# A hybrid decoder layer on eight cores: channel-major residual, measured durations in the order's planner, late weights in new places

## What is computed

```
x = x + 0.5 * swiglu(rmsnorm(x, ffn1_norm), w1, w3, w2)        # D_FF 2816
h = rmsnorm(x, mix_norm)
u = h @ w_in                                                   # q k v gate lru_x lru_gate
y_ret = (silu(g_ret) * head_groupnorm(retention(rotary(q), rotary(k), v))) @ w_ret_o
y_lru = (rg_lru(causal_conv(x_lru)) * gelu(g_lru)) @ w_lru_o
gates = sigmoid(h @ w_branch_gate + b)
x = x + (gates[:D] * y_ret + gates[D:] * y_lru) @ w_out
p = softmax((rmsnorm(x, xattn_norm) @ w_xq) (m @ w_xk)^T / 16) # m = rmsnorm(mem), 256 tokens, 4 heads
x = x + (p (m @ w_xv)) @ w_xo
x = x + 0.5 * swiglu(rmsnorm(x, ffn2_norm), ...)
out = rmsnorm(x, final_norm)
```

## Time and profile before

| | us |
|---|---|
| three runs, median (lowest to highest) | 1814.12 (1813.47 to 1816.82) |
| span of the profiled execution, slowest core | 1809.7 |
| spans of the eight cores | 1798.3 to 1809.7 |
| PE busy | 1713.9 (95%) |
| DVE, ACT, POOL busy | 879.6, 660.4, 374.8 |

### The profile page before, as it was taken

How to read it: one execution, slowest core, us unless ns; L and a number is a source line. 1 busy time by engine, 2 the same in 40 slices (tenths; PEclk the granted TensorE clock), 3 DMA queues, 4 the chain that set the end, 5 groups by cost and what they waited for, 6 DMA issues and landing times.

```text
span 1809.7 us, 24417 instructions; the slowest of 8 cores (1798.3 to 1809.7 us)
## 1 busy us (share of the span) xinstructions
PE 1713.9 (95%) x8432; PEld 815.1 (45%) x8600; DVE 879.6 (49%) x1309; ACT 660.4 (36%) x1016; POOL 374.8 (21%) x423
## 2 busy tenths in 40 slices
...
GB/s 223 133 60 75 105 153 83 28 78 122 146 257 16 85 54 58 49 43 49 36 24 47 110 197 78 83 191 48 12 71 12 49 45 1 70 36 12 7 93 93
DMA packets 56263, 141.62 MB, mean 78 GB/s; under 512 B 5968, under 2 KB 18256, under 8 KB 54096
## 3 DMA queue, kind: packets, MB, share of 16 engines
...
HBM read 168.87 MB, written 33.55 MB: 112 GB/s over the span
## 4 chain that ended last, share of the span: by engine, by line
PE 89%; DMA 3%; DVE 3%; issue 2%; ACT 1%; POOL 0%; SPq 0%; DVEq 0%; ACTq 0%; POOLq 0%
PE bank L636 86%; PE bank L847 1%; DMA X<-x 1%; DMA TW_107<-w_tail 1%; DMA X<-park 1%; DVE HB L839 0%; DMA XW<-w_xqT 0%; PE bank L1299 0%; DVE XC L1132 0%; DVE SC L1262 0%; PE bank L1302 0%; DVE T_88 L1210 0%; DVE T_88 L1208 0%; DVE SG L1315 0%; PE bank L1331 0%
## 5 line engine op out<-in xcount | busy, mean ns | idle before, releaser
L636 PE MATMUL bank<-hT,W_45 128*128 128x512 bf16 x2755 | 613.4, 379 | 4.3 <-DVE hT L855 1.0
L636 PEld LDWEIGHTS bank<-hT,W_45 128*128 128x128 bf16 x2816 | 275.2, 98 | 328.9 <-issue 2.8
L652 ACT ACTIVATE STMP<-bank 128x512 f32<-128x512 f32 x176 | 104.9, 596 | 597.0 <-PE bank L636 573.9
L636 PE MATMUL bank<-W_46,HID 128*128 128x512 bf16 x1378 | 311.1, 380 | 2.7 <-DVE HID L918 1.0
L936 DVE SCALAR_TENSOR_TENSOR X<-bank,X 128x512 f32<-128x512 f32 x256 | 175.3, 689 | 190.9 <-PE bank L636 174.2
L918 DVE TENSOR_TENSOR HID<-bank,STMP 128x512 bf16<-128x512 f32 x176 | 120.1, 690 | 299.7 <-PE bank L636 288.8
L636 PEld LDWEIGHTS bank<-W_46,HID 128*128 128x128 bf16 x1408 | 137.3, 98 | 164.3 <-issue 3.1
L652 ACT ACTIVATE JUNK<-X 128x1024 bf16<-128x1024 f32 x80 | 84.4, 1055 | 130.6 <-DVE X L936 63.7
L831 POOL TENSOR_TENSOR stat<-stat,cst 128x1 f32<-128x1 f32 x82 | 48.0, 587 | 351.7 <-DVE stat L830 349.7
L636 PE MATMUL bank<-hT,LW 128*128 128x512 bf16 x500 | 114.9, 382 | 0.6
L665 POOL DMA_DIRECT2D W_45<-f_w x44 | 23.9, 547 | 404.0 <-PE bank L636 393.9
...
## 6 DMA issues: line engine op xcount, KB each, us to landing
W_45<-f_w POOLq DMA_DIRECT2D x44, 512.0 KB, 7.1
...
X<-x SPq DMA_DIRECT2D x16, 512.0 KB, 10.6
park<-X SPq DMA_DIRECT2D x16, 512.0 KB, 9.0
X<-park SPq DMA_DIRECT2D x16, 512.0 KB, 23.1
out<-OST SPq DMA_DIRECT2D x16, 512.0 KB, 2.6
...
```

The source lines that it names most:

```text
L636: ins = e.matmul(out_ap, l, r, start=(start and i == 0), stop=(stop and i == n - 1), skip_group_check=skip)
L652: P.add("act", lambda e: e.activation(out, in_, func, **kw), reads=reads, writes=writes, cost=act_cost(n, nap), tab=tab)
```

## The change

- **X is channel-major**: `x`, `mem`, `out` and `park` come in a layout of [block, 128 channels, 8, 512 tokens]. `norm` works on a block of 512 tokens (256 for the first two blocks of FFN 1, for `mem`, and for the last block of the final norm): Squares to bf16 on ACT, sums over the 8 channel groups on DVE, one matmul with ones for the sum over partitions, Ln and Exp on ACT into `RSN`, eight products with a gain column on DVE (L995) straight into `hT`. No transposes, no gain rows, no POOL step. `w2`, `w_out` and the attention output have the weights stationary and the tokens moving.
- **Cross-attention**: scores with tokens on partitions, a maximum per head (DVE), Exp with an accumulated sum per head and 128 tokens (ACT, 256 wide), reciprocal and four products on DVE, eight transposes on PE, an eviction on ACT (`PX`); four buffers of `PEX` instead of two.
- **First loads**: the first two blocks of x come as four quarters of 256 tokens, alternating with the weights of FFN 1; the first hidden blocks are computed on halves of 256 tokens in the order of the expected arrivals. The last `w2` of FFN 2 is split into two halves of tokens. A one-element Exp loads ACT's table before the first norm, another after the last Silu.
- **Places**: `RW0` and `RW1` change sides (96 KB and 0), `TW` lies at 120, 0, 4, 64 and 68 KB, `GIN` and `WO` move too; the loads of `WO` wait for a `TW`.
- **Planner**: hand-overs are counted by pairs of engines (480 ns from PE to ACT, 530 to DVE, and 200 more for anything that PE waits for), operations on one engine overlap a little, DVE and POOL exclude each other in some operations, `TAB_HOLD` is 0, a bank class may be dealt out up to 6 ahead, and 24 passes are made, each with keys from a pass backward over the last plan; the shortest is kept.
- `NRAW` is 0 and `FPOOL` is empty, so the code for `raw`, `keep`, `later` and `pool_chunks` adds nothing.

```diff
 SEM_NS = 70.0
-DMA_NS_PER_B = 1.0 / 215.0
+LAT = {("pe", "act"): 480.0, ("pe", "dve"): 530.0, ("pe", "pool"): 900.0, ("pe", "sp"): 450.0, ("pe", "pe"): 0.0}
+LAT_TO = {"pe": 115.0, "act": 95.0, "dve": 103.0, "pool": 145.0, "sp": 80.0}
+OVL = {"pe": 0.0, "act": 46.0, "dve": 79.0, "pool": 31.0, "sp": 0.0}
+MARGIN = {"pe": 200.0}
+DMA_NS_PER_B = 1.0 / 285.0
 DMA_LAT = 2500.0
 TAB_NS = 1283.0
-TAB_HOLD = 600.0
+TAB_HOLD = 0.0
+LOOK = 6
+PASSES = 24
...
     def schedule(self):
+        best = None
+        keys = None
+        for it in range(PASSES):
+            plan = self.one_pass(keys)
+            if best is None or self.span < best[0]:
+                best = (self.span, plan, self.order)
+            keys = self.backward(plan)
+        self.span, plan, self.order = best
+        return plan
...
+    def lat_of(self, d, s):
+        k = LAT.get((d.eng, s.eng))
+        if k is None:
+            k = LAT_TO[s.eng]
+        if d.eng == "dve" and s.eng == "dve" or d.eng == "act" and s.eng == "act" or d.eng == "pool" and s.eng == "pool":
+            k = 20.0
+        if s.eng == "pe" and d.eng != "pe":
+            k += MARGIN["pe"]
+        return k
...
-            if c.q[c.i] != v or not free or c.use >= c.cap:
+            if not free or len(c.held) >= c.cap:
                 return None
+            if c.q[0] != v:
+                if v not in c.q[:c.look]:
+                    return None
+                if len(c.held) + max(0, c.keep - sum(1 for x in c.held if x < c.q[0])) >= c.cap:
+                    return None
...
-    def rstd_of(src_ap, src_hs, j):
...
-        jk = JUNK.v()
-        act(jk.ap, src_ap, AF.Square, src_hs, jk.hs + hs, D, accum=s[:, 0:1])
-        dve(lambda e: e.tensor_scalar(s[:, 1:2], s[:, 0:1], 1.0 / D, EPS, ALU.mult, ALU.add), hs, hs, 1)
-        pool(lambda e: e.tensor_tensor(s[:, 2:3], s[:, 1:2], cc(2), ALU.pow), hs + cst.hs, hs, 550)
...
+        for q in range(0 if ones else 4):
+            x = src(2 * q, 2)
+            d = part(2 * q, 2)
+            act(d.ap, x.ap, AF.Square, x.hs, d.hs, 2 * n)
+            if q:
+                dve(lambda e, d=d: e.tensor_tensor(acc.ap, acc.ap, d.ap, ALU.add), acc.hs + d.hs, acc.hs, 2 * n, 0.55)
...
+        r = keep if keep is not None else RSN.v((i % 2) * TB, n)
+        act(r.ap, banks[b][:, 0:n], AF.Ln, [hbk[b]] + cst.hs, r.hs, n, tab=S_LN, bias=cc(0), scale=1.0 / D)
+        act(r.ap, r.ap, AF.Exp, r.hs, r.hs, n, tab=S_EXP, scale=-0.5)
...
+                x = src(c, 1)
+                d = dst(c)
...
+                else:
+                    dve(lambda e, x=x, d=d, g=gc(c): e.scalar_tensor_tensor(d.ap, x.ap, g, r.ap, ALU.mult, ALU.mult),
+                        x.hs + r.hs + gcol.hs + list(after), d.hs, n, 1.148)
...
-                        pairs.append((hd.ap[:, j * 128:(j + 1) * 128], w.ap[:, half * 512:(half + 1) * 512]))
+                        pairs.append((w.ap[:, oc * 128:(oc + 1) * 128], hd.ap))
...
                     pend = [a for a in pend if a[1] % 2 not in [tb % 2 for tb in tbs]]
+                    first = halves and g == 0 and tbs[0] == 0
+                    if first:
+                        units = []
+                        for m, t in itertools.product(range(G), range(2)):
+                            if m < FULL[t]:
+                                units += [(m, t, 256 * hf, 256, 2 * t + hf) for hf in range(2)]
+                            else:
+                                units.append((m, t, 0, TB, 2 * t + 1))
+                        units.sort(key=lambda u: (max(ARR_W[u[0]], ARR_X[u[4]]), u))
...
-    GIN = [A.buf("GIN%d" % i, o * KB, F16, 2 * T) for i, o in enumerate((112, 64, 72, 80))]
-    TW = [A.buf("TW%d" % i, o * KB, BF16, 2 * KC * 128) for i, o in enumerate((120, 88, 92, 112, 116))]
-    WO = A.buf("WO", 96 * KB, BF16, KC * D)
+    GIN = [A.buf("GIN%d" % i, o * KB, F16, 2 * T) for i, o in enumerate((16, 8, 72, 80))]
+    TW = [A.buf("TW%d" % i, o * KB, BF16, 2 * KC * 128) for i, o in enumerate((120, 0, 4, 64, 68))]
+    WO = [A.buf("WO%d" % i, o * KB, BF16, D) for i, o in enumerate((88, 90, 92, 94, 164, 166, 198, 200))]
...
-            if oc == 2:
-                for k in range(KC):
-                    v = WO.v(k * D, D)
-                    wdma(v.ap, wout_d[k], [], v.hs, 128 * D * 4)
-            if oc == 4:
-                sp_dma(MS.v().ap, m_dr, h_md, MS.v().hs, 128 * 8192 * 2)
+            if oc == 6:
+                sp_dma(MS.v().ap, m_dr, h_md + tw(7).v().hs, MS.v().hs, 128 * 8192 * 2)
...
-                act(ri.ap, banks[b][:, :], AF.Ln, [hbk[b]], ri.hs, TB, tab=S_LN)
-                act(ri.ap, ri.ap, AF.Exp, ri.hs, ri.hs, TB, tab=S_EXP, scale=-1.0)
...
-                dve(lambda e, px=px, pe_=pe_, rib=rib: e.tensor_tensor(px.ap, pe_.ap, rib, ALU.mult), pe_.hs + ri.hs, px.hs, 2 * TB)
+                    dve(lambda e, b=b, hp=hp, sm=sm: e.tensor_reduce(sm[:, 2 * hp:2 * hp + 2],
+                                                                     banks[b][:, :].rearrange("p (h m) -> p h m", h=2),
+                                                                     mybir.AxisListType.X, ALU.max), [hbk[b]], hs, 512)
+                dve(lambda e, sm=sm: e.tensor_scalar(sm[:, 4:8], sm[:, 0:4], -1.0 / 16.0, None, ALU.mult), hs, hs, 4)
+                for h in range(4):
+                    act(pe_.ap[:, h * MEM:(h + 1) * MEM], banks[bs[h // 2]][:, (h % 2) * MEM:(h % 2 + 1) * MEM], AF.Exp,
+                        [hbk[bs[h // 2]]] + hs, pe_.hs + hs, MEM, tab=S_EXP, bias=sm[:, 4 + h:5 + h], scale=1.0 / 16.0,
+                        accum=sm[:, 8 + h:9 + h])
+                dve(lambda e, sm=sm: e.reciprocal(sm[:, 12:16], sm[:, 8:12]), hs, hs, 4)
+                for h in range(4):
+                    pv = pe_.ap[:, h * MEM:(h + 1) * MEM]
+                    dve(lambda e, pv=pv, sm=sm, h=h: e.tensor_scalar(pv, pv, sm[:, 12 + h:13 + h], None, ALU.mult),
+                        pe_.hs + hs, pe_.hs, MEM, 0.5)
+                b = bkt.next()
...
+                P.add("pe", tr, reads=pe_.hs + identb.hs, writes=[hbk[b]], cost=8 * 64)
+                px = PX.v((tb % 2) * KC * TB, KC, TB)
+                src = bv.rearrange("p (c t) -> p c t", c=KC)
+                act(px.ap[:, :, j * 128:(j + 1) * 128], src, AF.Copy, [hbk[b]], px.hs, D)
...
+    P.boost = 1e9
+    xa = load_x(0, 0, 4, 0, 256)
+    P.boost = 9.8e8
+    xb = load_x(0, 4, 4, 0, 256)
+    P.boost = 9.7e8
+    xq = [load_x(0, 0, 8, 256, 256)]
+    P.boost = 9.6e8
+    sp_dma(gcol.ap, gains_d, [], gcol.hs, 128 * 6 * KC * 4)
+    wh = [f1.load13(xa)]
...
+    P.boost = 7.9e8
+    wh.append(f1.load13(xq[0]))
+    P.boost = 7.8e8
+    xq.append(load_x(1, 0, 8, 0, 256, wh[0]))
+    P.boost = 7.7e8
+    wh.append(f1.load13(wh[1]))
+    P.boost = 7.6e8
+    wh.append(f1.load13(xq[1]))
```

More of the change, by code:

```diff
@@ L515 @@
 STAGE = 99
+W2BOOST = 3e4
+FPOOL = ((), (), ())
+NRAW = 0
+FULL = (2, 4)
+FLOOK = 1
+ARR_W = (3.0, 4.0, 6.0, 7.0, 9.0, 10.0)
+ARR_X = tuple(a + (0.5 if q < NRAW else 2.5) for q, a in enumerate((1.0, 2.0, 5.0, 8.0)))
 def build(stage=None):
@@ new lines, in norm_x, with final_block, done @@
+    def norm_x(tb, gain, bk, o=0, n=TB, **kw):
+        norm(lambda c, m: xv(tb, c, m, o, n), gain, lambda c: hTb.v((tb * KC + c) * TB + o, n), n, bk, **kw)
+    def final_block(tb, bk, o, n):
+        def done(c):
+            if c % 2:
+                v = xv(tb, c - 1, 2, o, n)
+                h_out.append(H("out"))
+                sp_dma(out_d[tb, :, c - 1:c + 1, o:o + n], v.ap, v.hs, [h_out[-1]], 128 * 2 * n * 4)
+        P.boost = 1e6
+        norm(lambda c, m: xv(tb, c, m, o, n), "final_norm", lambda c: xv(tb, c, 1, o, n), n, bk,
+             ones=n < TB, pool_chunks=FPOOL[2 if n == TB else 0 if o == 0 else 1], done=done)
+        P.boost = 0.0
@@ L920, in w2 @@
-        def w2(self, ms, tb, bk2, post):
-            G = len(ms)
+            if raw is None:
+                rh = [hTb.v((tb * KC + k) * TB + o, n) for k in range(KC)]
+            else:
+                rh = [raw[0](k) for k in range(KC)]
+            hs = sum([r.hs for r in rh], [])
+            for r, b in ((0, b1), (1, b3)):
+                mm_group(banks[b][:, 0:n], b, [(w.ap[:, r, k, :], rh[k].ap) for k in range(KC)], w.hs + hs, cols=n)
+            if n < TB:
+                s = STMP.v((self.st % 6) * 256, n)
+                self.st += 1
+            else:
+                self.st += self.st % 2
+                s = STMP.v((self.st % 6) * 256, n)
+                self.st += 2
@@ new lines, in w13 @@
+            if raw is None:
+                act(s.ap, banks[b1][:, 0:n], AF.Silu, [hbk[b1]], s.hs, n, tab=S_SILU)
+            else:
+                r = raw[1]
+                dve(lambda e: e.tensor_tensor(s.ap, banks[b1][:, 0:n], r.ap, ALU.mult), [hbk[b1]] + r.hs, s.hs, n)
+                act(s.ap, s.ap, AF.Silu, s.hs, s.hs, n, tab=S_SILU)
+                dve(lambda e: e.tensor_tensor(s.ap, s.ap, r.ap, ALU.mult), s.hs + r.hs, s.hs, n)
```

(16 more changed lines are left out.)

541 lines of the change are left out of this document (311 added, 230 removed).

## The result

The changed kernel takes **1715.1 us** (median; 1714.5 to 1715.4) beside 1813.8 for the kernel before: ratio 0.9457 (0.9441 to 0.9473), 98.7 us less. The forecast was 1738, the range 1708 to 1776. What came is the rival "nearly no holes" (1716), to which I had given one chance in ten. The profiled execution spans 1713.2 us on its slowest core, 1.9 less than the median; the eight cores lie between 1709.5 and 1713.2 at a granted clock of 0.998 or 0.999.

The account below looks back on a forecast made before the run. PE's own work at full rate, plus what keeps PE from working, was taken to bound the kernel. The terms summed to -75.5 us, a span of 1734, plus 4.4 to the median: 1738 us, range 1708 to 1776.

Parts of the forecast that it names:

- nearly no holes: Rival, 10%: the new plan fills the mixers as the FFNs are filled, 1.2% idle, giving 1716 us.
- PE's work: Whole kernel: PE's own matmuls and transposes fall from 1694 to 1671.6 us and this counts in full, -22.5 us.
- the start: Before the first FFN matmul: it comes at 15.5 us instead of 30.6, waiting only for 1 MB of x, -12.5 us.
- the end: After the last matmul: the final norm's chain takes some 6.5 us where the old took 5.5, +0.5 us.
- The order of the mixers: 500 to 1000 and 1100 to 1200 us: realistic hand-overs and backward-pass keys fill two thirds of PE's waits, -30 us.
- the order gives nothing: Rival, 16%: mixer holes come from real chains, not the plan's 70 ns; 1768 us, or 1776 with a late tail load.
- The tail's weights: 1000 to 1100 us: the tail weight's load gets 14 or more of its 16 us landing covered by other work, -14 us.
- The 30 to 100 us: Early first FFN, paced by 1 MB loads: its holes and clock loss shrink a little, -3 us.
- Attention: Cross-attention: DVE stays below PE but nearer, +4 us (0 to +12).
- norms and tables: DVE and ACT: norms cost the same, hidden; 75 table loads instead of 44, mostly where ACT is idle, +2 us.
- The softmax chain: Slower rival, 2%: in the attention each tile's 6.5 us chain lies bare, 104 us for 16, giving 1842 us.
- The clock: Slower rival, 0.5%: with PE denser the granted clock falls in the full stretches; at 0.91 it gives 1824 us.

Follow-up runs that it names:

- the attention's run: The changed kernel with the old kernel's cross-attention (transposed scores, sums by ones, Ln and Exp) in the new layout: 1717.5 us, ratio 0.9476.

## Why the prediction was right, and where it was not

The span can be split without double counting by the matmuls' starts: ahead of the first FFN matmul, PE's work, behind the last matmul, and the holes and half clock between. Before it was 28 + 1694 + 11 + 77 (the prediction's own split, in this order). Now it is 19.6 (20.04 less four ones-matmuls) + 1671.6 + 8.0 (last matmul from 1704.93 for 0.27) + 14.

| us | predicted | found |
|---|---|---|
| PE's work | -22.5 | -22.5 |
| ahead of the first FFN matmul | -12.5 | -8.4 |
| holes and half clock between | -41 (-3 -14 -30 +4 +2) | -63 |
| behind the last matmul | +0.5 | -3 |
| span | -75.5 | -96.5 |

The mechanism held in the main: PE's own work shrank as counted, and most of the gain is holes that closed. The sum was short by 21 us. What closed, read by stretches below, adds up to some 72 us and not 63: holes and half clock count some time twice, and from 20 to 30 us PE now has 1.0 us of holes and 1.7 of half rate that it did not have before; the rest of the difference I cannot place. The rival "nearly no holes" met the time within 1 us partly by luck: it put nothing on the tail's other 6 us, nor on the attention and tables that cost nothing, and missed that the start would be 4 us short.

**PE's work** holds: the trace has the 7273, 793 and 280 matmuls, and they stand as far apart as before: 48 take 10.52 us.

```profile
1681.78 10.52 PE L758 MATMUL bank<-hT,W 128*128 128x512 bf16 x48
```

The program alone gave 38 us under the new plan (1753.2 to 1715.1). PE's work makes 22.5 of them, the start 3.8 (the old program under the new plan has 25.62 less 2.2 of transposes ahead), the end 2.6 (10.6 to 8.0). The other 9 are about what that run still waits for loads of `XW` (7.1 and 1.4 us), for which the changed kernel does not wait:

```profile
PE bank L737 <- DMA XW<-w_xo: 7.1, 2, 5.2
PE bank L737 <- DMA XW<-w_xqT: 1.4, 1, 1.4
```

Under the old plan it gave nothing: the term is real only where PE has no holes into which it can be lost. I had written "this counts in full" without that condition.

**The order of the mixers** is the term most off, as a size. I put the bounds at 0 and 42, "two thirds", -30. The earlier trace rows lose 32 + 3 to holes and 10 to the clock; after the change 3 is left, so 42, the upper bound. The reason I gave for filling them, that all other engines were at 64% or less, was good for all of them, and I had no row that spoke for a third to stay. My picture of how was also incomplete. I named the hand-overs of 70 ns; with overlap and margin they are worth 11 us of the 54 of all values. Bank look-ahead with the table hold is worth 22, and the 24 passes 31. The prediction mentioned the passes in half a sentence and the look-ahead not at all. The rival "the order gives nothing" (16%) is refuted by the old program under the new plan, 59 us.

**The tail's weights**, -14: the stretch 1000 to 1100 gained its whole 20, but mostly not by the step I gave. Places and load times are worth 7.6 us under the new plan, by the run with the old ones. The stretch itself is full with the old places too, in that run and with the old program under the new plan, where no wait for a `TW` is left at all. The plan does that; with the old places the first `TW` is used at 960 us, not 1005, and the wait behind it is 2.6 us and not 7.6.

**What I left out**: the holes of 5 us in 100 to 500 and of 3 from 1200 on also closed, nearly all of the 8. I had named them only in the rival.

**The start**, -12.5. The first two x loads were there at about the forecast's time (last Square from 8.23), Ln and Exp were done at 11.8. I left one operand of the products out: the gain columns, 3.7 us. Even without them the products, interleaved with other tokens' sums, end at 17.2. And the term was worth less than it said: the run with the gains first takes off 2.6 us and gives them back. Part of the gain is no merit of the new loads: the new plan alone brings the old program's start from 28 to 23.4. The 30 to 100 us went as forecast, 4.1 + 1.4 to 2.8.

**Attention** (+4) and **norms and tables** (+2) cost nothing that shows: 460.00 busy of 460 from 1200 on, and the attention's run gives 2.4 for the new form, within the noise. The 75 table loads are there, 1283 ns each, hidden:

```profile
L774 ACT ACT_TABLE_LOAD x75 | 96.2, 1283 | 33.9 <-PE bank L758 22.4 <-DVE HID L1081 3.8 <-DVE cst L822 3.0
```

The drain of 1.38 us by which the Trainium skill (ScalarE: Activation LUTs, "What ACT_TABLE_LOAD costs") would have made this term +4 is not seen. **The end**: -3 instead of +0.5. Split into token halves, the last `w2` has the ones-matmuls of its norm between its own matmuls, and only two Squares are left behind it; I had sized the chain and not seen that most of it moves ahead.

**The slower rivals.** The softmax chain did not lie bare (1100 to 1200 is 100.00 busy, with DVE at 79). The clock did not fall: in the profiled execution it was 0.998 or more on all eight cores with PE 98% busy, so the rule of 13/16 that I cited from the Trainium skill (TensorE: Matmul & The Clock Gate, Part 1) does not show here.

**The range.** Two of its sums are off as written. 1708 is what all terms give at their favourable bounds (30 us less); those of the mixers and the start alone, 12 and 3.5, give 1722. And with order and tail both at nothing 44 us come back, 1782 and not 1776. So the 1715.1 that came lies in the range only because the favourable ends of the other terms were in it.
